# A mixture-of-experts kernel: the further rows of four experts gathered, turned and split together

## The reference, cut to what matters

```python
scores = sigmoid(x @ w_router)                  # [1024, 64]
top_e  = the 8 best experts of each token       # within the 4 best groups of 8
w      = scores[top_e] / sum * 2.5
for each expert e, for its tokens in blocks:
    h  = silu(xb @ w_gate[e]) * (xb @ w_up[e])  # [rows, 1024] @ [1024, 256]
    yb = (h @ w_down[e]) * w                    # [rows, 256] @ [256, 1024]
    acc[rows] += yb
out = LayerNorm(alpha * x + acc + shared_expert(x))
```

## Time and profile before

| | |
|---|---|
| median of 3 executions | 1635.14 us (1634.45 to 1638.62) |
| profiled execution | 1633.34 us, its span 1631.7 us |
| PE busy | 1567.5 us (96%) |
| DVE busy | 1178.9 us (72%) |
| ACT busy | 1033.5 us (63%) |
| POOL busy | 506.6 us (31%) |
| granted TensorE clock, mean | 0.98 |

### The profile page before, as it was taken

How to read it: one execution, slowest core, us unless ns; L and a number is a source line. 1 busy time by engine, 2 the same in 40 slices (tenths; PEclk the granted TensorE clock), 3 DMA queues, 4 the chain that set the end, 5 groups by cost and what they waited for, 6 DMA issues and landing times.

```text
span 1631.7 us, 32189 instructions
## 1 busy us (share of the span) xinstructions
PE 1567.5 (96%) x8246; PEld 1309.8 (80%) x8247; DVE 1178.9 (72%) x2037; ACT 1033.5 (63%) x1706; POOL 506.6 (31%) x495
## 2 busy tenths in 40 slices
PE   6999999999999999989999999999999999999986
PEld 6897888888887788778888888888888888888763
DVE  4215777777777788836877787777876787888866
ACT  3215666666666654526777787767776777878754
POOL 0000000000000125532554454543454454454426
PEclk9999999999999999999999999999999999999995
DMA  7223322222123434557999999999999999999987
GB/s 246 91 81 91 72 53 65 58 64 71 45 71 104 161 144 146 221 192 267 330 312 323 304 354 366 342 289 274 333 328 286 286 358 327 352 367 362 368 250 281
DMA packets 161321, 368.63 MB, mean 226 GB/s; under 512 B 53010, under 2 KB 73490, under 8 KB 161266
## 3 DMA queue, kind: packets, MB, share of 16 engines
q1 hardware_dynamic: 136272, 284.21, 49.7%
q0 software_dynamic: 24992, 83.73, 19.7%
HBM read 294.39 MB, written 65.11 MB: 220 GB/s over the span
## 4 chain that ended last, share of the span: by engine, by line
PE 73%; DVE 8%; DMA 7%; issue 5%; ACT 3%; ACTq 2%; POOL 1%; SPq 0%; DVEq 0%; POOLq 0%
PE bank_pair L1031 6%; PE bank_pair L1025 6%; PE bank_pair L1028 6%; DMA sums_scratch<-ys,sidx 6%; PE q_ps L91 4%; PE q_ps L93 4%; PE q_ps L92 4%; PE out_ps L916 4%; PE k_ps L894 3%; PE out_ps L1084 3%; PE out_ps L1085 3%; PE q_ps L1015 3%; PE k_ps L1052 2%; PE k_ps L1053 2%; PE k_ps L1060 2%
## 5 line engine op out<-in xcount | busy, mean ns | idle before, releaser
L1918 DVE TENSOR_TENSOR gu_lo<-raw_gu,gu_hi 128x1024 fp32r<-128x1024 f32 x260 | 306.4, 1220 | 28.0 <-ACT gu_hi L1396 27.8
L1396 ACT CAST gu_hi<-raw_gu 128x1024 fp32r<-128x1024 f32 x260 | 253.6, 1049 | 7.1 <-DMA raw_gu<-in_moe_w_up_dram 7.1
L1025 PE MATMUL bank_pair<-gu_hi,xb_hi 128*128 128x512 f32 x576 | 233.9, 406 | 5.3 <-DVE gu_lo L1918 3.9
L1028 PE MATMUL bank_pair<-gu_lo,xb_hi 128*128 128x512 f32 x576 | 227.7, 395 | 0.0
L682 POOL DMA_INDIRECT sums_scratch<-ys,sidx x63 | 120.8, 1917 | 152.9 <-DMA sums_scratch<-ys,sidx 118.9
L1918 DVE TENSOR_TENSOR dn_lo<-raw_dn,dn_hi 128x1024 fp32r<-128x1024 f32 x130 | 152.6, 1213 | 2.8 <-ACT dn_hi L1396 2.3
L1031 PE MATMUL bank_pair<-gu_hi,xb_lo 128*128 128x512 f32 x576 | 144.0, 392 | 3.8 <-DVE xb_lo L1922 3.8
L1025 PEld LDWEIGHTS bank_pair<-gu_hi,xb_hi 128*128 128x128 f32 x576 | 110.6, 192 | 28.6 <-issue 5.8
L613 POOL IOTA e<- 128x64 f32 x1 | 0.2, 185 | 427.5 <-DVE xs L1714 427.5
L1396 ACT CAST dn_hi<-raw_dn 128x1024 fp32r<-128x1024 f32 x130 | 130.0, 1052 | 4.2 <-DMA raw_dn<-in_moe_w_down_dram 4.2
L1301 ACT CAST pt_hi<-k_ps 128x512 fp32r<-128x512 f32 (+1 forms) x192 | 85.8, 482 | 73.5 <-PE k_ps L894 72.8
(11 more groups left out here) (307 smaller groups left out, 3967.5 us busy)
## 6 DMA issues: line engine op xcount, KB each, us to landing
raw_gu<-in_moe_w_gate_dram SPq DMA_DIRECT2D x128, 512.0 KB, 7.0
raw_gu<-in_moe_w_up_dram SPq DMA_DIRECT2D x128, 512.0 KB, 9.1
raw_dn<-in_moe_w_down_dram SPq DMA_DIRECT2D x128, 512.0 KB, 8.7
wqk<-in_fox_w_in_dram SPq DMA_DIRECT2D x66, 128.0 KB, 2.5
v_scratch<-v_out SPq DMA_DIRECT2D x32, 256.0 KB, 2.8
va<-v_scratch SPq DMA_DIRECT2D x16, 512.0 KB, 4.6
fin<-sums_scratch SPq DMA_DIRECT2D x16, 512.0 KB, 9.5
xs<-in_x_dram SPq DMA_DIRECT2D x8, 512.0 KB, 7.3
```

What stands on the lines that cost most here:

```text
L1025: i = pe.matmul(o3, xb_hi[s][:, c], g_hi[:, :, c], start=c == 0, stop=False, skip_group_check=True)
L1028: pe.matmul(o3, xb_hi[s][:, c], g_lo[:, :, c], start=False, stop=False, skip_group_check=True)
L1396: a.copy(hi, raw).then_inc(S[done], 1)
L1918: dve.tensor_tensor(lo, raw, hi, ALU.subtract).then_inc(S[lo_ok], 1)
```

## The change

The further blocks of four neighbouring experts (32 rows each) are gathered by one indirect DMA of 128 rows. It is bounded: places of the table that hold no token are skipped. The 128 rows are turned at once into `k_ps` in the middle of `gate_up` of every fourth expert (an even round; a round is two experts), cast and subtracted in one instruction each, into a wider `xo` of 256 columns per chunk: for each of the four experts 32 high and 32 low columns. A stationary operand is 128 of these columns, so the expert's results stand in rows 0 to 63 and the other rows are not used. On odd rounds `second_pair` moves the columns of experts three and four to the place of one and two. A second or later further block of an expert is gathered after the first is done (`gather_again`). The table is stored by block instead of by expert, and only its first 128 columns are loaded. Several semaphores are merged.

```diff
@@ table and running sums
-            tab = sb("tab", [P, TAB], I32, c=m)
+            tab = sb("tab", [P, 2 * E], I32, c=m)
+            xo = sb("xo", [P, DC * 2 * P], F32R, c=m)
+            xo_of = xo[:, 0:DC * 2 * P].rearrange("p (c j s r) -> p c j s r", j=FOUR, s=2, r=XR)
...
+                step(dve.tensor_scalar(u[:], nblk_i[1][:], float(-(P // XR) - 1), 0.0, ALU.add, ALU.max))
...          (the same running sum as for `earlier`)
+                dve.tensor_copy(again[:, 1:E + 1], u[:]).then_inc(S["extra_ok"], 1)
@@ DVE, last block of the shared expert
+                    dve.wait_ge(S["c_loads"], 64)
+                    for j in range(FOUR):
+                        dve.tensor_copy(fidx[j * XR:(j + 1) * XR], tab[0:XR, E + j:2 * E:FOUR]).then_inc(S["extra_ok"], 1)
+                    dve.memset(xgx[:], 0.0).then_inc(S["extra_ok"], 1)
@@ POOL
+            def gather_four(n):
+                if static(n) and n == 0:
+                    pool.wait_ge(S["extra_ok"], 4 + FOUR)
+                else:
+                    pool.wait_ge(S["fx_lo_ok"], FOUR * n - 2)
+                stand(pool)
+                g.tensor_copy(fidx_g[:], fidx[:, ds(n, 1)]).then_inc(idx_ok[2], 1)
+                pool.wait_ge(idx_ok[2], n + 1)
+                stand(pool)
+                g.indirect_dma_start(out=xgx[:], out_offset=None, in_=rows_dram,
+                                     in_offset=bass.IndirectOffsetOnAxis(ap=fidx_g[:, 0:1], axis=0), bounds_check=T - 1, oob_is_err=False
+                                     ).then_inc(S["fx_in"], 16)
...          (called once before the experts, behind the stores L711, and in expert 4n + 1 for n + 1)
-            f0, f1 = further_of(0), further_of(1)
-            with pool.If(f0 > 0):
-                gather_further(0, 0, 0, 0)
...
@@ PE
-            def gate_up(s, w, names, n):
+            def gate_up(s, w, names, n, between=None):
...
+                    if between and c == DC // 2 - 1:
+                        between()
...
+            def turn_four(n, m):
+                pe.wait_ge(S["fx_in"], 16 * n + 16)
+                pe.wait_ge(S["scaled"], m - 1)
+                stand(pe)
+                turn_rows(xgx, k_ps).then_inc(S["fx_turned"], 1)
...
+                def rows_of_four():
+                    with pe.If(odd < 1):
+                        turn_four(four, m)
+                between = rows_of_four if par == 0 and not static(odd) else None
...
+                if par == 0:
+                    pe.wait_ge(S["fx_lo_ok"], e + 2)
+                    stand(pe)
                 with pe.If(nx > 0):
...
-                    pe.wait_ge(S["ht_lo_ok"], m)
-                    turn_further(par, xi + nx - 1)
                     down(m - 1, par, e + 1)
...
-                    gate_up_further(w, xi + nx - 1)
+                    gate_up_further(w, par, xi + nx - 1)
@@ ACT
-                        next_gate_up(m, e, par)
+                        next_gate_up(m, e, par, range(G_PIECES - 1))
+                    if par == 0 and not static(odd):
+                        with act.If(odd < 1):
+                            rows_of_four_hi(four)
...
+                    if pos != "last":
+                        next_gate_up(m, e, par, range(G_PIECES - 1, G_PIECES))
...
-                    with act.If(nx > 0):
-                        further_rows_hi(after - 1)
                     down_weights(range(D_PIECES))
@@ DVE
+            def rows_of_four_lo(n):
+                dve.wait_ge(S["fx_hi_ok"], n + 1)
+                q = xo[:, 0:DC * 2 * P].rearrange("p (q s r) -> p q s r", s=2, r=XR)
+                dve.tensor_tensor(q[:, :, 1], k_ps[:].rearrange("p (q r) -> p q r", r=XR), q[:, :, 0], ALU.subtract).then_inc(S["fx_lo_ok"], 1)
+                for j in range(FOUR):
+                    i = dve.tensor_copy(w_four[:, j:j + 1], xgx[j * XR:(j + 1) * XR, ds(FOUR * n + (D + j), 1)])
+                i.then_inc(S["fx_lo_ok"], 1)
+
+            def second_pair(m):
+                dve.wait_ge(S["started"], m + 1)
+                stand(dve)
+                v = xo[:].rearrange("p (c h r) -> p c h r", c=DC, h=2)
+                dve.tensor_copy(v[:, :, 0], v[:, :, 1]).then_inc(S["fx_lo_ok"], 2)
...          (DVE's list of an expert, with a further block before)
                     next_weights(range(G_PIECES - 1))
+                    if par == 0 and static(odd):
+                        second_pair(m)
+                    elif par == 0:
+                        with dve.If(odd < 1):
+                            rows_of_four_lo(four)
+                        with dve.If(odd > 0):
+                            second_pair(m)
                     further_h_lo(xi - 1)
...          (without one: the same lines between `next_weights` and `h_of`)
-                        further_rows_lo(par, e, after - 1)
+                        first_weights(par, odd, four)
                     down_weights(range(D_PIECES))
```

More of the change, by code:

```diff
@@ L711, in _, with expert @@
                     pool.dma_start(sums[0][(b - 1) * P:b * P, :], ys[(b - 1) % 2][:]).then_inc(sent[(b - 1) % 2], 16)
+            gather_four(0)
             gather(0, 2, 1, [(S["w_ok"], 1)])
-            f0, f1 = further_of(0), further_of(1)
-            with pool.If(f0 > 0):
-                gather_further(0, 0, 0, 0)
[L716 to L720, removed]
+            def expert(e, par, odd, four, pos, ahead=True):
                 xi, nx = earlier_of(e), further_of(e)
                 ends = pos == "last" and par == 1
-                f1 = None if ends else further_of(e + 1)
-                f2 = None if pos == "last" else further_of(e + 2)
                 if ahead:
                     gather(1 - par, e + 3, (e + 2 + par) // 2, [(S["w_ok"], e + 2)])
+                if par == 1 and not static(odd):
+                    with pool.If(odd < 1):
+                        gather_four(four + 1)
+                elif par == 1 and odd == 0 and four + 1 < E // FOUR:
+                    gather_four(four + 1)
                 if ends:
@@ L1163, in _, with expert @@
                     logits(TT - 1)
-            def expert(e, par, last=False):
+            def expert(e, par, odd, four, last=False):
                 w = 1 - par
@@ L1220, in _ @@
                 for par in range(2):
-                    expert(2 * i + par, par)
-            expert(E - 2, 0)
-            expert(E - 1, 1, last=True)
+                    expert(2 * i + par, par, i & 1, i // 2)
+            for par in range(2):
+                expert(E - 2 + par, par, 1, E // FOUR - 1, last=par == 1)
         @block.scalar
@@ L1514, in load_counts, with expert @@
                 return [act.value_load(earlier[0:1, ds(e + k, 1)], min_val=0, max_val=E * TAB_BLOCKS) for k in range(4)]
-            def expert(e, par, pos, counts):
+            def expert(e, par, odd, four, pos, counts):
                 m = SH + e
@@ L1587, in _ @@
             counts = load_counts(0)
-            expert(0, 0, "first", counts)
-            expert(1, 1, "", counts)
+            expert(0, 0, 0, 0, "first", counts)
+            expert(1, 1, 0, 0, "", counts)
             with act.Fori(1, E // 2 - 1) as i:
@@ L2007, in load_counts, with expert @@
                 return [dve.value_load(earlier[0:1, ds(e + k, 1)], min_val=0, max_val=E * TAB_BLOCKS) for k in range(4)]
-            def expert(e, par, counts, last=False):
+            def expert(e, par, odd, four, counts, last=False):
                 m = SH + e
@@ L2042, in expert @@
                     next_weights(range(G_PIECES - 1))
+                    if par == 0 and static(odd):
+                        second_pair(m)
+                    elif par == 0:
+                        with dve.If(odd < 1):
+                            rows_of_four_lo(four)
+                        with dve.If(odd > 0):
+                            second_pair(m)
                     if last:
-                        dve.tensor_copy(tok_f[:], tab[:, e * TAB_BLOCKS:e * TAB_BLOCKS + 1]).then_inc(S["place_step"], 1)
+                        dve.tensor_copy(tok_f[:], tab[:, e:e + 1]).then_inc(S["place_step"], 1)
                     h_of(m)
@@ L2055, in expert @@
                         further_y(xi + k)
-                    further_rows_lo(par, e, after - 1)
+                        again_lo(e, par, n + k)
                 with dve.If(nx < 2):
                     with dve.If(nx > 0):
-                        further_rows_lo(par, e, after - 1)
+                        first_weights(par, odd, four)
                     down_weights(range(D_PIECES))
```

245 lines of the change are left out of this document (140 added, 105 removed).

## The result

| | before | changed |
|---|---|---|
| median | 1635.45 us (4 runs) | 1686.29 us (4 runs, 1685.39 to 1690.16) |
| profiled execution, its span | 1633.34, 1631.7 us | 1690.16, 1688.3 us |

The change makes the kernel slower by 3.2%: ratio 1.0316, 95% interval 1.0299 to 1.0334. I had said 1649, range 1633 to 1664: the sign was right, the size was a third of what came.

The account below looks back on a forecast made before the run. The prediction took TensorE as the bound (busy 96% of the span): +15.0 us up to expert 54, +4.9 in the last ten, less 1.2 and 4.1, gave +14.6 and a forecast of 1649 us, range 1633 to 1664.

Parts of the forecast that it names:

- Odd experts: Odd experts with a further block only gain, by dropping the small turn: 17 x -1.2 = -20.4 us up to expert 54.
- The new waits: TensorE waits before `down` in even experts with no block before: 2.8 us on even rounds, 3.05 on odd.
- the first gather's: In expert 0's `gate_up` TensorE waits 6.7 us for `gather_four(0)`; with the turn's 1.15, +7.9 us.
- a TensorE wait added is time added: Up to expert 53 TensorE is busy 716.5 of 723 us, so each added wait costs its length.
- Expert 48's kind: Even rounds, no block before, none of its own (12 and 48): 1.15 + 2.8 - 0.65 = +3.3 us each, +6.6 together.
- none before, both rounds: Even experts with no further block in the expert before, on even and odd rounds: together +16.5 us.
- expert 54 to expert 63: Last ten experts: TensorE's additions make it the first to set the pace, +4.9 us.
- the end behind them: Behind the last experts: expert 63 gives 1.2 us back, and POOL's last add goes out when ready, -4.1.
- the forecast's 100.9 us: TensorE's nine steps in the last ten experts: 86.2 us of own work, 96.0 measured before, 100.9 with the additions.
- the wait for `ho`: Even rounds, a block before: TensorE comes 1.15 us later, DVE 1.7 later, so 0.4 of waiting, 1.55 with `turn_four`.
- dearer control: Rival, chance 0.15: added branches and register steps lengthen loop bodies, 8 to 13 us, `second_pair` 6 more; 1659, at worst 1668.
- Covered waits: Rival, chance 0.12: DVE and ACT run ahead, so neither `fx_lo_ok` nor the first gather costs anything; -26.5, about 1609.

Follow-up runs that it names:

- b1: Kernel before plus one TensorE wait in even experts, behind `turn_next`, for DVE's third `gu_lo` quarter: 1679.03 us, ratio 1.0271.
- b3: Kernel before plus a TensorE wait for DVE's fourth `gu_lo` quarter in even experts, with 15 unused products ahead of it: 1678.85 us, ratio 1.0270.
- v1: Changed kernel with first gather issued earlier, `second_pair` ahead of the `gu_lo` quarters, four blocks cast and subtracted behind the first weight quarter: 1623.74 us, ratio 0.9934.
- v3: v2, plus DVE splitting the third weight quarter behind `ho` and `hh` in even experts with a block before them: 1615.21 us, ratio 0.9871.
- b2: Kernel before plus one TensorE wait in even experts, behind `turn_next`, for DVE's fourth `gu_lo` quarter, unfilled: 1702.11 us, ratio 1.0413.
- v2: v1, plus DVE's preparation for the further rows and `gather_four(0)` moved one shared block earlier: 1617.33 us, ratio 0.9895.

## Why the prediction was wrong

Right: the direction; that no expert has two blocks; and the steps one by one. Odd experts are 1.2 us shorter (14.17 to 12.97 in expert 9). `second_pair` takes 0.69 (forecast 0.75):

```profile
790.42 3.50 DVE L1983 TENSOR_TENSOR gu_lo<-raw_gu,gu_hi 128x1024 fp32r<-128x1024 f32 x3
793.83 0.69 DVE L2013 CAST xo<-xo 128x1024 fp32r<-128x1024 f32 x1
```

`turn_four` lengthens a step by 0.93 (1.15, the bounds were 0.9 and 1.2). Experts 10, 18, 26, 34, 38 and 50 (on odd rounds, a block before) take 0.55 longer without a block of their own and 0.7 less with one (forecast +0.65 and -0.55). The new waits are 3.24 on average (2.8 to 3.05), the first gather's 6.6 (6.7).

Wrong: the price of a wait. The prediction sets out with "a TensorE wait added is time added", and its step is "TensorE wants `down` at 1402.62 ... 2.8 us of waiting. Expert 48's kind then pays 1.15 + 2.8 - 0.65". It prices a wait at its length. The runs show that the products behind it must be paid too, where the clock falls: 1.9 us more for a wait of 3.2 on average. All three kinds of wait of the sum (none before, both rounds; expert 0) were priced so. The missing 42.0 us, span against span (forecast +14.6, measured +56.6), from start to start of the last eight products of `gate_up`:

| part | forecast | measured | beyond |
|---|---|---|---|
| ahead of expert 0 | 0 | +4.7 | 4.7 |
| last shared block to expert 0 | +7.9 | +10.2 | 2.3, its slow products (5.1 us at 0.50) |
| expert 0 to expert 54 | +7.1 | +31.2 | 24.1: low clock 18.6; 5.5 more |
| expert 54 to expert 63 | +4.9 | +13.9 | 9.0: low clock 6.8; 2.2 more |
| the end behind them | -5.3 | -3.4 | 1.9 |

The low clock is 2.3 + 18.6 + 6.8 = 28 of the 42. In the last ten it counts in full: the forecast's 100.9 us were nine steps at the full clock, and 109.8 were measured, 103.0 without the low clock. (The kernel before had 3.1 us of it there, within its 96.0.) The 5.5 between experts 0 and 54 come out of the single steps, low clock taken off: the ten even experts with none before take 4.3 more than forecast in all, 0.2 to 0.7 each; the ten experts of even rounds with a block before (4, 8, 16, 20 and so on) take 0.78 more for the wait for `ho` (0.53 of it shows as idle time), not 0.4, and 0.93 for `turn_four`, not 1.15, together 1.6 over; the six of odd rounds are 0.7 under.

The other 2.2 of the last ten, the 1.9 at the end and the 4.7 ahead of expert 0 are not settled. The kernels before and b1 to b3, with one code there, reach that point at 746.5 to 750.5, the changed kernel and the experiments on it at 748.7 to 754.8. The profiled execution of the changed kernel was also 3.9 us over its median. So part of the 4.7 may be spread between executions. I did not try the second running sum by itself.

The rivals: *dearer control* gave 1659 to 1668 and was wrong in kind, as v1 shows: with all of the added branches in it, the experts' own work comes to 676.6 us in the stage (689.5 - 11.4 - 1.5), against 699.0 before. That is -22.4; the 29 small turns of this stage and 13 turns of four give -34.8 + 15.0 = -19.8 at the forecast's prices, and -22.7 with `turn_four` at the 0.93 measured. Steps without a new wait say the same: 11.43 us from expert 5 to 6, 21 to 22 and 45 to 46 in both kernels, and 9.34 to 9.38 where it was 9.34 to 9.35. *Covered waits* (1609) was not this kernel, but the path to it was open: v3 reaches 1615.

The profile of before had a hint: the granted clock is 1.00 up to expert 53 and 0.96 behind it, where loads come late and TensorE waits. I read the waits there and did not ask what the clock did. Between expert 0 and expert 63 that trace shows one fall, behind a wait of 2.75 us:

```profile
1554.53 0.61 PE L1039 MATMUL bank_pair<-ident,hh 128*128 128x128 f32 x2 [2.75 <-DVE hh L1926]
1554.80:1561.50 6.70, 6.18 (x16) 4.62 (x16) 5.35 (x7) 5.44 (x7) 2.25 (x3) 0.50 1.04 337
```

## What to carry to other kernels

When a change adds many waits of 2.3 us or more to a TensorE that is never idle, price them at 1.5 to 1.6 times their length: on average 2.6 us cost 3.9, 3.2 cost 5.1, 4.0 cost 6.0. A single one of 2.3 to 3.4 us cost anything from its length to some 3 us more. Look at how many instructions and how many busy microseconds a stage has: 134 fewer in the same busy time were the sign of the lower clock here. And before judging an idea by its first order of instructions, move what ends each new wait to the earliest place where its inputs exist; here that turned +3.2% into -1.3% with the same arithmetic.

## What the runs showed that I had not expected

- Unused work made a kernel faster. b3 does 225 products more than b2 and takes 23 us less.
- Short waits did the clock no harm: in v3's stage 5.5 us of idle time, no stop over 0.9 us, lose 0.0 us; in v2 11.6 us, none over 0.9, lose 0.0.
- The fall need not come at once. In b2, behind 3.54 us of idle array, the eight transposes and two products still run at the full rate; from 792.97 on the products start 0.43 apart, and 0.23 apart again from 796.5:

```profile
791.07 1.04 PE L1074 MATMUL bank_pair<-ident,x_rows 32*128 32x32 f32 x8 [3.54 <-DMA x_rows<-rows_scratch,gidx]
792.04 0.50 PE L1052 MATMUL k_ps<-dn_hi,ht_hi 128*128 128x512 f32 x1
792.37 0.39 PE L1053 MATMUL k_ps<-dn_lo,ht_hi 128*128 128x512 f32 x1
792.60 0.57 PE L1052 MATMUL k_ps<-dn_hi,ht_hi 128*128 128x512 f32 x1
792.97 0.63 PE L1053 MATMUL k_ps<-dn_lo,ht_hi 128*128 128x512 f32 x1
```

In b3, where this wait is filled, the clock is 1.00 over the same products. So the slow stretch belongs to the wait ahead of it even where fast products lie between.
